# Attention's queries and keys in two rounded parts, written by the scan and loaded as such, and the first scores ahead of the first values' turn

## What is computed

```python
q = _rmsnorm(q, q_norm); k = _rmsnorm(k, k_norm)
Ft = jnp.cumsum(jax.nn.log_sigmoid(f_logit + b_f), axis=1)
s = q @ k.T * Dh**-0.5 + Ft[query] - Ft[key]     # causal
p = softmax(s);  y = p @ v
```

## Time and profile before

| | |
|---|---|
| runs | 3154.23, 3163.36, 3169.47 us (median 3163.36) |
| profiled execution: its time / its span | 3179.65 us / 3177.8 us |
| PE busy / PEld busy | 2972.4 us (94%) / 2180.4 us (69%) |
| DVE / ACT / POOL busy | 1468.2 (46%) / 1133.4 (36%) / 979.7 us (31%) |
| mean granted TensorE clock | 0.946 of 2.4 GHz |
| layer 1: scan / forgetting attention | about 440 to 1050 us / 1050 to 1348 us of the span |
| layer 2: scan / forgetting attention | about 2031 to 2645 us / 2645 to 2948 us of the span |

### The profile page before, as it was taken

How to read it: one execution, slowest core, us unless ns; L and a number is a source line. 1 busy time by engine, 2 the same in 40 slices (tenths; PEclk the granted TensorE clock), 3 DMA queues, 4 the chain that set the end, 5 groups by cost and what they waited for, 6 DMA issues and landing times. The chain is left out here.

```text
span 3177.8 us, 67901 instructions
## 1 busy us (share of the span) xinstructions
PE 2972.4 (94%) x26644; PEld 2180.4 (69%) x26644; DVE 1468.2 (46%) x2204; ACT 1133.4 (36%) x2284; POOL 979.7 (31%) x890
## 2 busy tenths in 40 slices
PE   7999989999999789889889999899999997999799
PEld 6867867777777444367668678677777775444577
DVE  5127733322222577567451277333222224766674
ACT  5004433333333344633250044333333333446332
POOL 5101112344444224532141011123444442236221
PEclk9999999999999679989989999999999996799899
DMA  5224543344443211266332245434444432112663
GB/s 153 77 75 154 165 115 97 111 120 125 121 122 104 68 37 40 74 197 203 127 119 76 75 154 162 116 92 116 121 120 118 123 108 71 37 38 64 199 202 110
DMA packets 421183, 358.01 MB, mean 113 GB/s; under 512 B 127624, under 2 KB 358280, under 8 KB 420872
## 3 DMA queue, kind: packets, MB, share of 16 engines
q1 hardware_dynamic: 350696, 320.14, 33.5%
q10 hardware_dynamic: 70176, 33.59, 4.1%
HBM read 222.84 MB, written 130.84 MB: 111 GB/s over the span
## 5 line engine op out<-in xcount | busy, mean ns | idle before, releaser
L129 PE MATMUL ch_acc<-h_hi,ch_w_hi 128*128 128x512 f32 (+1 forms) x2048 | 822.7, 402 | 21.2 <-PEq L126 20.4
L135 PE MATMUL ch_acc<-h_hi,ch_w_lo 128*128 128x512 f32 (+1 forms) x2048 | 828.5, 405 | 0.0
L133 PE MATMUL ch_acc<-h_lo,ch_w_hi 128*128 128x512 f32 (+1 forms) x2048 | 825.8, 403 | 0.2 <-issue 0.2
L129 PEld LDWEIGHTS ch_acc<-h_hi,ch_w_hi 128*128 128x128 f32 (+1 forms) x2048 | 381.7, 186 | 108.5 <-issue 24.0
L133 PEld LDWEIGHTS ch_acc<-h_lo,ch_w_hi 128*128 128x128 f32 (+1 forms) x2048 | 381.5, 186 | 98.1 <-issue 11.5
L135 PEld LDWEIGHTS ch_acc<-h_hi,ch_w_lo 128*128 128x128 f32 (+1 forms) x2048 | 380.6, 186 | 89.1 <-issue 0.3
L115 POOL TENSOR_TENSOR ch_w_lo<-ch_raw,ch_w_hi 128x1024 fp32r<-128x1024 f32 (+1 forms) x62 | 149.1, 2404 | 744.8 <-POOLq L114 744.8
L1680 ACT ACTIVATE fx_prob<-fx_ST 128x512 f32<-128x512 f32 (+3 forms) x320 | 156.2, 530 | 201.1 <-PE fx_ST L1535 96.3
L1927 PE MATMUL so_acc<-ea_wo_hi,so_m_hi 128*128 128x512 f32 x512 | 207.4, 405 | 6.8 <-POOL so_m_lo L1862 6.8
L1929 PE MATMUL so_acc<-ea_wo_lo,so_m_hi 128*128 128x512 f32 x512 | 203.7, 398 | 0.0
L1599 DVE TENSOR_REDUCE fx_nm<-fx_SS 128x2 f32<-128x1024 f32 (+3 forms) x160 | 167.6, 1060 | 76.5 <-PE fx_SS L1510 63.8
(11 more groups left out here) (285 smaller groups left out, 4932.1 us busy)
## 6 DMA issues: line engine op xcount, KB each, us to landing
projT<-ch_stage SPq DMA_DIRECT2D x248, 256.0 KB
ch_raw<-w_in ACTq DMA_DIRECT2D x62, 512.0 KB, 5.5
pj_xb<-x SPq DMA_DIRECT2D x32, 512.0 KB, 4.6
so_stage<-x SPq DMA_DIRECT2D x64, 256.0 KB, 3.4
rp_pre<-projT SPq DMA_DIRECT2D x16, 899.5 KB, 7.7
rs_qx<-projT SPq DMA_DIRECT2D x112, 128.0 KB, 3.3
projT<-rs_qx SPq DMA_DIRECT2D x112, 128.0 KB, 1.8
rs_cs<-rope SPq DMA_DIRECT2D x48, 256.0 KB, 3.7
```

What stands on the lines that cost most here:

```text
L129: ins = M(acc, self.w_hi[q][:, k, 0:m], self.h_hi[:, k, cols], start=(k == 0), stop=False)
L133: M(acc, self.w_hi[q][:, k, 0:m], self.h_lo[:, k, cols], start=False, stop=False)
L135: ins = M(acc, self.w_lo[q][:, k, 0:m], self.h_hi[:, k, cols], start=False, stop=(k == KC - 1))
```

## The change

The normalized queries and keys of the forgetting attention are no longer stored in place. In a plain unit POOL makes the high part `qh` (one more multiplication, with a rounding output), the full product as before, and then subtracts one from the other (one more operation); SP stores both parts to a new array `qk` (two stores for one). The attention loads from `qk` straight into `Q1`, `Q2`, `K1`, `K2`: per block and head three loads for the first scores (semaphore `a_in`) and four more (`b_in`), and no engine splits. All pieces `r` are gone from the plan, the values' turns stand elsewhere, ACT issues the loads of two constants, and POOL fills the rows of ones in three pieces with a signal each (`one_rdy`).

```diff
@@ phase_rwkv_scan, SP
             def store_norm(u):
                 e, (r, b) = u % 3, norms[u]
                 sp.wait_ge(s["q_out"], u + 1)
-                sp.dma_start(projT[row_of[r]:...], qx[e][:]).then_inc(q_st[e], 16)
+                if turned(u):
+                    sp.dma_start(projT[row_of[r]:...], qx[e][:]).then_inc(q_st[e], 16)
+                else:
+                    for part, buf in ((0, qh[plain.index(u) % 2][:].bitcast(F32)), (1, qx[e][:])):
+                        row = (r // 2 * 2 + part) * GW + r % 2 * 128
+                        sp.dma_start(qk[row:row + 128, b * UB:(b + 1) * UB], buf).then_inc(q_st[e], 16)
@@ phase_rwkv_scan, POOL, scale(u)
                 pool.wait_ge(s["q_fac"], u + 1)
+                if not turned(u):
+                    f = plain.index(u)
+                    if f > 1:
+                        pool.wait_ge(q_st[plain[f - 2] % 3], stores[plain[f - 2]])
+                    G.tensor_tensor(qh[f % 2][:], x[:], qr[u % 2][:], ALU.mult)
                 G.tensor_tensor(x[:], x[:], qr[u % 2][:], ALU.mult)
+                if not turned(u):
+                    pool.drain()
+                    G.tensor_tensor(x[:].bitcast(F32R), x[:], qh[f % 2][:].bitcast(F32), ALU.subtract)
                 pool.drain().then_inc(s["q_out"], 1)
@@ phase_fox, plan()
-            beside = [("r", 0, i) for i in range(4)] + [("v", 0, 0)]
-            splits = [(R, [("r", B, i) for B in bs for i in range(4)]) for R, bs in ((0, (1,)), (1, (2,)), (2, (3, 4)), (3, (5, 6, 7)))]
+            beside = []
+            splits = {R: [("v", B, 0) for B in bs] for R, bs in ((0, (0, 1)), (1, (2,)), (2, (3, 4)), (3, (5, 6, 7)))}
...
-                    if todo and i >= n - len(splits[R]):
+                    if todo and i >= n - (2 if R else 1) * len(todo):
                         beside.append(todo.pop(0))
@@ phase_fox, SP
-            sp.dma_start(ident[:], consts[:, 0:128]).then_inc(s["c_in"], 16)
-            sp.dma_start(cm[:], consts[:, 1024:1152]).then_inc(s["c_in"], 16)
...
-                if R > 1:
-                    sp.wait_ge(s["k_split"], R - 1)
-                    sp.wait_ge(s["d_split"], R - 1)
-                    sp.wait_ge(s["p_split"], R - 1)
+                qh, ql, kh, kl = (qk[n * GW:(n + 1) * GW, cols] for n in range(4))
+                rows_of = [slice((2 * p + h) * HD, (2 * p + h + 1) * HD) for h in two]
                 for h in two:
-                    r = (2 * p + h) * HD
-                    sp.dma_start(rq[h][:, R % 2], projT[R_FQ + r:...]).then_inc(raw_in[R % 2], 16)
-                    sp.dma_start(rk[h][:, R % 2], projT[R_FK + r:...]).then_inc(raw_in[R % 2], 16)
-                    sp.dma_start(K2[p][h][HD:KX, cols].bitcast(F32), fa[...]).then_inc(raw_in[R % 2], 16)
+                    sp.dma_start(Q2[p][h][0:HD, cols].bitcast(F32), qh[rows_of[h]]).then_inc(a_in[R], 16)
+                    sp.dma_start(K2[p][h][0:HD, cols].bitcast(F32), kh[rows_of[h]]).then_inc(a_in[R], 16)
+                    sp.dma_start(K2[p][h][HD:KX, cols].bitcast(F32), fa[...]).then_inc(a_in[R], 16)
+                for h in two:
+                    for buf, lo, hi in ((Q1[p][h], ql, qh), (K1[p][h], kh, kl)):
+                        sp.dma_start(buf[0:HD, cols].bitcast(F32), lo[rows_of[h]]).then_inc(b_in[R], 16)
+                        sp.dma_start(buf[HD:128, cols].bitcast(F32), hi[rows_of[h]]).then_inc(b_in[R], 16)
                 if R > 1:
                     sp.wait_ge(s["lt_rdy"], lt_n["v", R - 2])
                 sp.dma_start(rv[:, R % 2], projT[R_FV + 2 * p * HD:...]).then_inc(v_in[R % 2], 16)
                 if R == 5:
                     store(0)
@@ phase_fox, POOL
-            for p in two:
+            for p, a, n in ((0, 0, TB), (0, TB, T - TB), (1, 0, T)):
                 for h in two:
-                    G.tensor_copy(Q2[p][h][HD:KX, :], LS[HD:KX, 0, 0:1].to_broadcast([KX - HD, T]))
-            pool.drain().then_inc(s["c_rdy"], 1)
+                    G.tensor_copy(Q2[p][h][HD:KX, a:a + n], LS[HD:KX, 0, 0:1].to_broadcast([KX - HD, n]))
+                pool.drain().then_inc(s["one_rdy"], 1)
@@ phase_fox, DVE (ACT's Q2, K2, K1 copies and POOL's Q1 copy go in the same way)
-                if k == "r" and x > 1:
-                    V.tensor_tensor(Q1[p][h][0:HD, c], rq[h][:, R % 2], Q2[p][h][0:HD, c].bitcast(F32), ALU.subtract)
-                    ins = V.tensor_tensor(K1[p][h][HD:128, c], rk[h][:, R % 2], K2[p][h][0:HD, c].bitcast(F32), ALU.subtract)
```

More of the change, by code:

```diff
@@ L625, in phase_rwkv_scan @@
         cs = P.sb("cs", [128, 2, UB])
+        qh = [P.sb(f"qh{e}", [128, UB], F32R) for e in two]
         qr = [P.sb(f"qr{e}", [128, UB]) for e in two]
@@ L643, in turned @@
             return norms[u][0] > 3
+        plain = [u for u in range(NU) if not turned(u)]
+        stores = [sum(16 if turned(i) else 32 for i in range(u % 3, u + 1, 3)) for u in range(NU)]
         loads = [sum(96 if turned(i) else 16 for i in range(u % 3, u + 1, 3)) for u in range(NU)]
@@ L1275, in phase_fox @@
         rows = E.rows[:].rearrange("p k (e t) -> p k e t", e=2)
-        rq, rk, rv = [rows[0:HD, h] for h in two], [rows[0:HD, 2 + h] for h in two], rows[:, 4]
+        rv = rows[:, 4]
         high, low = (w[:].rearrange("p k c -> p (k c)") for w in (E.wo_hi, E.wo_lo))
@@ L1290, in phase_fox @@
         O, LT = P.ps("O", [128, TB]), P.ps("LT", [128, TB])
-        names = ("c_in", "c_rdy", "a_split", "k_split", "d_split", "p_split", "s_rdy", "m_rdy", "x_rdy",
-                 "lt_rdy", "lt_free", "l_rdy", "v_rdy", "t_rdy", "p_rdy", "pv_done", "add_d", "add_p", "rl_rdy", "o_free", "rl_free", "yo_rdy", "whi_rdy", "wlo_rdy", "th_rdy", "gate_d")
+        names = ("c_in", "c_rdy", "s_rdy", "m_rdy", "x_rdy",
+                 "lt_rdy", "lt_free", "l_rdy", "v_rdy", "t_rdy", "p_rdy", "pv_done", "add_d", "add_p", "rl_rdy", "o_free", "rl_free", "yo_rdy", "one_rdy", "whi_rdy", "wlo_rdy", "th_rdy", "gate_d")
         s = {n: P.sem(n) for n in names}
-        raw_in, v_in, yo_st = ([P.sem(f"{n}{b}") for b in two] for n in ("raw_in", "v_in", "yo_st"))
+        v_in, yo_st = ([P.sem(f"{n}{b}") for b in two] for n in ("v_in", "yo_st"))
+        a_in, b_in = ([P.sem(f"{n}{R}") for R in range(2 * NQ)] for n in ("a_in", "b_in"))
         block = ctx.enter_context(nc.Block())
@@ L1475, in _ @@
             pe.wait_ge(s["c_in"], 32)
-            pe.wait_ge(s["c_rdy"], 2)
+            pe.wait_ge(s["c_rdy"], 1)
             ns = nt = 0
@@ L1502, in _ @@
                     if x == 0:
-                        pe.wait_ge(s["a_split"], blocks[R])
-                        pe.wait_ge(raw_in[0], 96 * ((blocks[R] + 1) // 2))
-                        if blocks[R] > 1:
-                            pe.wait_ge(raw_in[1], 96 * (blocks[R] // 2))
+                        pe.wait_ge(s["one_rdy"], min(3, R + 1))
+                        for b in range(blocks[R]):
+                            pe.wait_ge(a_in[b], 96)
                     if ns > 1:
@@ L1524, in _ @@
                     if x == 0:
-                        pe.wait_ge(s["k_split"], blocks[R])
-                        pe.wait_ge(s["d_split"], blocks[R])
-                        pe.wait_ge(s["p_split"], blocks[R])
+                        for b in range(blocks[R]):
+                            pe.wait_ge(b_in[b], 128)
                         pe.wait_ge(s["l_rdy"], R + 1)
@@ L1644, in _ @@
             for k, R, x in order:
-                p, Q = divmod(R, NQ) if k in "rv" else rounds[R]
+                p, Q = divmod(R, NQ) if k == "v" else rounds[R]
                 c = slice(Q * TB, (Q + 1) * TB)
-                if k == "r" and x < 2:
-                    act.wait_ge(raw_in[R % 2], 96 * (R // 2 + 1))
-                    if R == 0:
-                        act.wait_ge(s["c_rdy"], 2)
-                    A(Q2[p][x][0:HD, c], rq[x][:, R % 2], ACT.Copy)
-                    ins = A(K2[p][x][0:HD, c], rk[x][:, R % 2], ACT.Copy)
-                    if x == 1:
-                        act.drain().then_inc(s["a_split"], 1)
-                if k == "r" and x == 2:
-                    for h in two:
-                        ins = A(K1[p][h][0:HD, c], rk[h][:, R % 2], ACT.Copy)
-                    ins.then_inc(s["k_split"], 1)
                 if k == "l":
```

42 lines of the change are left out of this document (14 added, 28 removed).

## The result

Twenty runs of each kernel on one chip: before has a median of 3158.77 us (3142.18 to 3169.47), the changed kernel 3171.56 us (3163.87 to 3181.42). The ratio is **1.0042, 95% interval 1.0029 to 1.0054: 12.8 us slower**, where 20 us less had been forecast. It is inside half a per cent, but on the other side of no change.

The account below looks back on a forecast made before the run. PE, busy 94% of the span, was taken as the bound. Start +4.0, attention stretch -48.7 and scan +24.2 summed to -20.5 us: 3143 us from a median of 3163.36, own range 3132 to 3156, whole range 3122 to 3180.

Parts of the forecast that it names:

- The scan, +24: Scan tiles 4 to 14: POOL's added work delays ACT's square, stopping PE 1.1 us, 22 times; bounds 0 and +35.
- The start, +2.0 per layer: Attention's start: PE waits for block 1's values instead of POOL's ones; +4 us in all, bounds -2 and +8.
- that 0.6: Attention's start: 0.6 us added because new loads are issued at 228 GB/s but 64-row loads ran at 215.
- The stretch at 1.2 GHz, 0: Attention, 1080 to 1112 and 2674.5 to 2706.6: PE already busy, nothing gained; bounds 0 and -16 per layer.
- The later blocks' loads, 0: Attention's later blocks: loads are in by about 1140, before the second pair's scores need them; no cost.
- The stretch behind it, -48.7: Attention after the 1.2 GHz stretch: idle falls to 3 us, clock returns to 1.00; both layers, bounds 0 and -54.7.
- the rival in which half stays: Attention behind the slow stretch: half of the clock's loss, 19.9 us, remains; 3163 us, chance 0.29.
- the slower one: Rival: clock falls as before, only idle time won, under 3.5 of 39.8 us regained; 3183 us, chance 0.14.
- the sign of a wrong forecast: Attention behind the slow stretch: a clock below 0.9, where near 1.00 was expected, would refute the forecast.

Follow-up runs that it names:

- the repeat: Kernel before, unchanged, run and profiled once more: 3159.82 us, ratio 0.9988.
- the scan alone: Changed kernel's scan with the attention function of the kernel before, output not the reference's: 3185.54 us, ratio 1.0085.
- no split: Changed kernel without POOL's extra multiplication and subtraction, zeros stored as the low part: 3142.94 us, ratio 0.9955.
- four roots: Changed kernel with four buffers for squares and roots, POOL copying the rounded product over the root: 3145.74 us, ratio 0.9956.
- early release: Changed kernel with ACT's square waiting for a signal after POOL's multiplications, not after the subtraction: 3147.07 us, ratio 0.9958.
- both repairs of the buffer's reuse: Two separate runs on the changed kernel: four root buffers, 3145.74 us; ACT's square released after POOL's multiplications, 3147.07 us.
- the merged 128-row loads: Changed kernel with four root buffers, values loaded earlier, and one 128-row load replacing two of 64: 3138.96 us, ratio 0.9938.
- short sums: Changed kernel with four root buffers and DVE's sum additions cut to 8 columns, output not the reference's: 3116.28 us, ratio 0.9855.
- the moved additions: POOL instead of DVE adds key tiles 2 and 6 in rounds 1 and 2: 3101.66 us on the values ahead, 3149.96 on the changed kernel.
- the values ahead: The merged 128-row loads, with later blocks' values loaded before the wide loads of the block ahead of them: 3130.43 us, ratio 0.9897.
- the kernel before with the moved sums: Kernel before, only edit: POOL instead of DVE adds key tiles 2 and 6 in rounds 1 and 2: 3134.04 us, ratio 0.994.
- loads in better order: Changed kernel with SP loading block 0's score loads, both values, block 1's score loads, then the others: 3170.33 us, ratio 1.0027.

## Why the prediction was wrong, point by point

The attention by parts, us per layer. The form before has six layers in three profiles (the first, the repeat, the scan alone), the changed form eight in four (the changed kernel, no split, four roots, early release):

| part | before: mean (range) | changed: mean (range) | difference |
|---|---|---|---|
| scan's end to tile 0.0 | 30.2 (30.1 to 30.5) | 34.4 (33.8 to 35.5) | +4.2 |
| tile 0.0 to 1.1 | 26.8 (22.0 to 27.8) | 24.0 (20.9 to 27.2) | -2.8 |
| tile 1.1 to 3.3 | 91.7 (87.4 to 97.0) | 80.3 (72.4 to 85.8) | -11.4 |
| tile 3.3 to the end | 148.8 | 148.7 | 0 |

That is -10.0 per layer, -20 in all. By the medians of the runs it is -14.0 (changed kernel against the scan alone) or -18.0 (no split against before), so the profiled executions, few as they are, are some us off.

*The scan, +24:* right in place, mechanism and size. The run of it alone gave +25, the stops are 22, and both repairs of the buffer's reuse took 24 to 26 us away again.

*The start, +2.0 per layer:* right in mechanism, half in size. The first score came at 10.0 us, as forecast, and PE then waited for both values' loads, but the maxima's first transpose came 3.6 and 5.1 us later than before and not 1.4 to 2. Two terms are at fault. SP took longer to issue: block 1's values went out 17.4 and 18.2 us after the first load, where my sum has 16.3, since one of the eight new loads took 0.62 to 0.74 us to issue, by the means of the four groups of eight; I had taken 0.575, less than the mean of the two values that I named, 0.60. And PE's turn of them came 3.8 and 4.5 us after that issue, where I took 2.8 to land and 0.6 on top. The row for that 0.6 (215 GB/s) was not one of 64-row loads alone: the 128-row load of block 1's values, issued at 1061.96 and landed 2.8 us later, was under way in it. I had bounded the sum at +8; it came to +8.4. The Trainium skill ("SBUF — State Buffer", Door 1: The DMA port swizzle) says that a transfer to 64 partitions reaches half of the ports. Here the merged 128-row loads moved 231 GB/s against 197, so doubling the ports gave far less than double here.

*The stretch at 1.2 GHz, 0:* -2.8 per layer. Its end moved: in four of eight layers the clock rose sooner and tiles 0.0 to 1.1 took 20.9 us instead of 27, as in one of six before (22.0). Why it rose sooner in those, no run shows.

*The later blocks' loads, 0:* right. From tile 3.3 to the end the attention takes 148.7 us in the new form and 148.8 in the old.

*The stretch behind it, -48.7:* this is the step that failed, and in it one half. The idle time went as I had it: 8.0 and 6.9 us before, 2.6 and 4.3 in the changed kernel, where I left 3 each. The clock did not come back. From tile 1.1 to 3.3 in the changed kernel:

```profile
1116.90:1196.90 80.00, 77.44 (x311) 39.93 (x310) 50.39 (x51) 28.44 (x56) 20.12 (x11) 0.83 0.22 68
2704.80:2790.60 85.80, 81.51 (x311) 41.85 (x310) 54.37 (x50) 28.18 (x55) 17.72 (x11) 0.79 0.18 53
```

77.44 x 0.17 + 81.51 x 0.21 = 30.3 us are lost to the clock; between the same marks of the first profile it was 43.6 (83.07 us busy at 0.79, 90.11 at 0.71). So 13 of some 40 us came back where I had put all of them (over all layers of the table, 15 of 39 for a pair of layers), and the clock was below the 0.9 that I had named as the sign of a wrong forecast. That is less than the rival in which half stays, and more than the 3.5 at which the slower one decides.

The argument was "PE's waits for maxima then mostly go; so does the reason for the clock's falls". The waits did mostly go, but one can be enough: 1.43 us at 1131, then 25 us at half clock, some 12 us for it. It need not be: in the second layer a wait of 1.45 us at 2773.6 brought no fall. Over all fifteen profiles, between tiles 1.1 and 3.3, PE waited 57 times for 0.96 us or more with the clock full; 38 times the clock fell, at the latest 2.1 us after the wait's end, and it fell nowhere else. The six layers without such a wait (short sums, and the moved additions on the values ahead and on the changed kernel) have no fall at all.

The comparison by which I excluded that the falls stay, the stretch from 1199 on with DVE at 98 of 137 us, took an average for a burst: where the clock falls, DVE is busy 3.8 of 4 us. I had the row that said so the earlier trace rows and used it for the rival alone. And I blamed the subtraction in the one stall that I showed, when a sum (2.41 us in the rows of 1127 above) stands in the same queue too. The short sums and the moved ones show it: DVE at 44 to 45 us from tile 1.1 to 3.3 and the stretch takes 65 to 71, DVE at 50 to 54 and it takes 72 to 86, DVE at 65 to 67 and it takes 87 to 97. The total is not what decides, though: the kernel before with the moved sums has DVE at 61 and takes 76 us in its second layer.

*The rivals:* the result lies between "half stays" (3163) and "falls as before" (3183). The forecast's base, a median of three runs, was 4.6 us above that of twenty, which moves each of them down by that. As for the difference: -20 + 25 is +5 and the runs say +12.8; some 4 of the other 8 us can be the choice of profiles. Those of the form before took 20.9 and 6.3 us more and 8.0 less than the medians of their runs, those of the changed form 1.5 and 2.5 more and 8.5 and 3.8 less; some 14 of the 20.9 lay outside the attentions, so by this estimate the attention's part is nearer -16. What makes the rest, no run here settles.

## What to carry to other kernels

Ask of a queue not only how long it is busy over a stretch, but how late its worst burst is: the share that is free on average does not help the one operation that PE waits for, and where a stop also costs clock, removing most of the stops can leave most of the cost (here 30 of 44 us) until the last long one is gone. When work is added ahead of a signal, see what the signal guards. Here it guarded a buffer and not the data, and a second pair of buffers, or the signal one instruction sooner, made the added work free. And try the cheapest way of relieving an engine first: one entry in a table of who adds gained some 20 us on either kernel, where rearranging what two phases store and load lost 12.8.

## What the runs showed of the hardware

- The full clock came back at different times over the same work: tiles 0.0 to 1.1 had a mean clock of 0.68 or 0.69 in four of eight layers of the changed form and 0.50 in the other four. With loads in better order PE began the first key tile 12.4 us sooner and did that work at clock 0.50; tile 1.1 came 2 us later in one layer (56.8 after 54.9) and 5 us sooner in the other (57.4 after 62.6).
- A wait of 1.4 us was followed by 25 us at half clock with PE never idle; of 57 waits of 0.96 us or more at full clock 38 were followed by a fall, and no fall came without one. In one of the eight layers (no split, first layer) the stretch had 5.1 us of idle time in four waits of 0.89 to 1.44 us and a clock of 0.97. Why that one was spared stays open.
- Loads of 64 and of 128 rows moved 197 and 231 GB/s here, and a load's landing grew from 3.0 to 6.6 us when it was made twice as large; a values' load behind them took 11.0 us to PE's turn instead of 3.3.
- POOL's rounding copy of 128x256 elements took 0.40 us, its multiplication of the same size 0.73, so that the split by copy and subtraction took 2.15 us from the multiplication's start to the subtraction's end (725.61 to 727.76) where the one by a second multiplication took 2.30 (727.31 to 729.61).
- POOL's additions beside DVE's did not take back what they gave: four more of them on POOL in a stretch (28.1 us busy instead of 19.9 and 17.9, from tile 1.1 to 3.3), and DVE's busy time fell from 50.6 and 54.4 to 44.2 us.
